# Six dense U rows a tile in the picking stage, and gathered dot products in three stages instead of one

## The reference, cut to what matters

```python
s = jnp.einsum('phcd,hckd->phck', qy, sub_keys)            # two scores tables a head
top_s, top_i = lax.top_k(s, PEER_TOPK)
cand_s = top_s[:, :, 0, :, None] + top_s[:, :, 1, None, :]
best_s, best_j = lax.top_k(cand_s.reshape(..., 256), 16)
gate = jax.nn.softmax(best_s, axis=-1)
act = jax.nn.gelu(jnp.einsum('pd,phkd->phk', xb, expert_u[experts]))
return jnp.einsum('phk,phkd->pd', gate * act, expert_v[experts])
```

## Time and profile before

| | us |
|---|---|
| median of 3 runs | 4415.63 (4413.09 to 4423.91) |
| profiled execution, whole | 4421.46 |
| span of its trace | 4419.7 |
| TensorE (matmul) busy | 3649.9 (83%) |
| VectorE busy | 2767.0 (63%) |
| ScalarE busy | 1112.5 (25%) |
| GpSimd busy | 825.4 (19%) |
| dot products L1116, 256 | 313.9, mean 1.226 each |
| gathers of U rows L1105, 256 | 317.3, mean 1.240 each |

### The profile page before, as it was taken

How to read it: one execution, slowest core, us unless ns; L and a number is a source line. 1 busy time by engine, 2 the same in 40 slices (tenths; PEclk the granted TensorE clock), 3 DMA queues, 4 the chain that set the end, 5 groups by cost and what they waited for, 6 DMA issues and landing times. The chain is left out here.

```text
span 4419.7 us, 61298 instructions
## 1 busy us (share of the span) xinstructions
PE 3649.9 (83%) x19108; PEld 3246.2 (73%) x19108; DVE 2767.0 (63%) x5265; ACT 1112.5 (25%) x1515; POOL 825.4 (19%) x900
## 2 busy tenths in 40 slices
PE   7499965555776588788788869999979999999996
PEld 1399965554655466788788869999977888888885
DVE  0322235655443566899777756666628888888887
ACT  0200014434321211222455542222222222222220
POOL 0000010111000000000000006666622222222221
PEclk9699986555777788898889989999989999999998
DMA  6222210000222100222365569999957777777775
GB/s 230 95 90 98 87 56 27 13 26 13 86 91 85 56 32 22 86 89 83 89 155 138 150 148 336 340 342 335 338 187 270 282 284 285 280 279 285 282 285 205
DMA packets 436796, 735.97 MB, mean 167 GB/s; under 512 B 222851, under 2 KB 274259, under 8 KB 433619
## 3 DMA queue, kind: packets, MB, share of 16 engines
q1 hardware_dynamic: 332052, 354.18, 24.2%
q0 software_dynamic: 98304, 368.10, 23.0%
q10 hardware_dynamic: 6336, 12.58, 0.8%
HBM read 605.75 MB, written 129.00 MB: 166 GB/s over the span
## 5 line engine op out<-in xcount | busy, mean ns | idle before, releaser
L329 PE MATMUL evo<-vhi,Hhi 128*128 128x512 f32 x1536 | 602.0, 392 | 47.0 <-DVE Hlo L1655 47.0
L330 PE MATMUL evo<-vlo,Hhi 128*128 128x512 f32 x1536 | 598.8, 390 | 0.0
L331 PE MATMUL evo<-vhi,Hlo 128*128 128x512 f32 x1536 | 598.4, 390 | 0.0
L329 PE MATMUL apar<-h2hi,auhir 128*128 128x384 f32 x1152 | 390.6, 339 | 53.2 <-DVEq L59 48.8
L1116 DVE SCALAR_TENSOR_TENSOR urow<-urow,nx 128x1024 f32<-128x1024 f32 x256 | 313.9, 1226 | 186.6 <-DMA urow<-in_expert_u_rows,fw_now 170.6
L1105 POOL DMA_INDIRECT vrow<-in_expert_v,fw_now x256 | 268.2, 1048 | 769.5 <-DVE acc L1125 757.8
L331 PE MATMUL apar<-h2hi,aulor 128*128 128x384 f32 x1152 | 386.3, 335 | 0.0
L330 PE MATMUL apar<-h2lo,auhir 128*128 128x384 f32 x1152 | 386.2, 335 | 0.0
L329 PEld LDWEIGHTS evo<-vhi,Hhi 128*128 128x128 f32 x1536 | 288.8, 188 | 119.5 <-issue 60.3
L1668 DVE TENSOR_TENSOR acc<-acc,evo 128x512 f32<-128x512 f32 x384 | 262.6, 684 | 167.4 <-PE evo L331 167.3
L1105 POOL DMA_INDIRECT urow<-in_expert_u_rows,fw_now x256 | 317.3, 1240 | 187.5 <-DVE urow L1116 87.2
(11 more groups left out here) (278 smaller groups left out, 7523.2 us busy)
## 6 DMA issues: line engine op xcount, KB each, us to landing
vraw<-in_expert_v SPq DMA_DIRECT2D x128, 512.0 KB
gates_dram<-gstage SPq DMA_DIRECT2D x12, 4096.0 KB, 21.9
ga<-ahead_dram SPq DMA_DIRECT2D x128, 384.0 KB, 5.3
gr<-gates_dram SPq DMA_DIRECT2D x128, 384.0 KB, 5.9
aurr<-in_expert_u POOLq DMA_DIRECT2D x72, 512.0 KB
ahead_dram<-ager SPq DMA_DIRECT2D x144, 192.0 KB
gwi<-in_w_in POOLq DMA_DIRECT2D x16, 1216.0 KB
proj_dram<-gyi SPq DMA_DIRECT2D x128, 152.0 KB, 1.8
```

The source lines that it names most:

```text
L329: pe.matmul(out, lhi, rhi, start=(k == 0), stop=False)
L330: pe.matmul(out, lhi, rlo, start=False, stop=False)
L331: return pe.matmul(out, llo, rhi, start=False, stop=(k == n - 1))
```

## The change

`ROWS_TILE` goes from 4 to 6, so 48 U rows lie in the picking stage and 56 are left for the last of the three stages; the gate stage keeps 24. Of the 256 items, 24 (four beside each dense tile) move to the picking stage, 48 (four a block) to the gate stage, and 184 stay, in 23 of 28 turns. The row buffers now exist in all three stages (two of them are halves of a tile of the norm stage).

```diff
-ROWS_TILE = 4
+ROWS_TILE = 6
 ROWS_BLOCK = 2
+ITEMS_BEST = DT * RING
+ITEMS_GATE = TD // 64 * RING
+ITEMS_REST = ITEMS - ITEMS_BEST - ITEMS_GATE
```

```diff
-                with pool.Fori(0, TT) as t:
-                    for j in range(R):
-                        A.load(pool, t * R + j, j % 2, row(t, j))
+                for j in range(2):
+                    A.load(pool, j, j, row(0, j))
+                for f in range(FEW):
+                    loads(f, range(R))
+                pool.wait_ge(index_done, FEW)
+
+                def pair(turn, last):
+                    for h in range(2):
+                        d = turn * 2 + h
+                        some = R - 2 if last and h else R
+                        few.choose(pool, d, h, d * RING)
+                        for i in range(RING):
+                            few.gather(pool, table, d, h, i)
+                            if i < some:
+                                loads(d + FEW, range(i, i + 1))
+                        loads(d + FEW, range(RING, some))
```

```diff
+                        if j == R // 2:
+                            act.wait_ge(bm_done, t + 1)
+                            act.activation(best[:, :, :], best[:, :, :], ACT.Exp).then_inc(be_done, 1)
...
+                    def dot(i):
+                        if one is None:
+                            few.dot_row(dve, (t + (-FEW)) * RING + i, i)
...
                                   + [dve.match_replace(cand2[:, h], best[:, h, 0:8], cand[:, h], NEG) for h in heads])
+                    cut(1)
+                    dot(0)
                     settle(dve, settled)
                     link.together([dve.max(best[:, h, 8:16], cand2[:, h]) for h in heads])
-                    cut(1)
                     settle(dve, settled)
                     link.together([dve.max_index(bj[:, h, 8:16], best[:, h, 8:16], cand2[:, h]) for h in heads])
+                    cut(2)
+                    dot(1)
...
                     link(dve.tensor_copy(rank[:, :, :], code[:, :, :]))
-                    cut(2)
...
                         link(dve.tensor_reduce(pick[:, c], eq[:, :, :, :].rearrange("p h k a -> p (h k) a"), AX, ALU.add))
+                        cut(3 + c)
+                        dot(2 + c)
...
-                    cut(3)
...
+                    cut(5)
```

```diff
+                    for half in range(2):
+                        b = turn * 2 + half
+                        batch = b + ITEMS_BEST // RING
+                        few.choose(pool, batch, half, batch * RING)
+                        for i in range(RING):
+                            few.gather(pool, table, batch, half, i)
+                            if i % 2 == 0 and not (last and half == 1):
+                                A.load(pool, b * 2 + (2 + i // 2), i // 2, b * 2 + (R0 + 2 + i // 2))
...
+                            if gi % RING == RING - 1:
+                                i = gi // RING
+                                few.dot_row(dve, b * RING + (ITEMS_BEST + i), i)
                             j, k = divmod(gi, PER)
-                            if k == 5 and not (last and half == 1 and j == ROWS_BLOCK - 1):
+                            if k == 4 and not (last and half == 1 and j == ROWS_BLOCK - 1):
                                 A.cut_low(link, b * 2 + (j + 1), 1 - j)
...
+                            if k == 0 and gi:
+                                A.gelu(act, b * 2 + (j - 1), 1)
+                            if k == 1 and not (last and half == 1 and j == ROWS_BLOCK - 1):
+                                A.cut_high(act, b * 2 + (j + 1), 1 - j, (b + j) * 16 + 16)
                             if k == 4:
                                 A.gelu(act, b * 2 + j, 0)
-                                if not (last and half == 1 and j == ROWS_BLOCK - 1):
-                                    A.cut_high(act, b * 2 + (j + 1), 1 - j, (b + j) * 16 + 16)
```

More of the change, by code:

```diff
@@ L1092, in __init__, with choose, gather, gather_all @@
         self.now_done = ctx.enter_context(nc.semaphore("fw_now_done"))
-    def gather(self, pool, table, first, batch, turn_batches, turn):
-        n = turn * (turn_batches * RING) + (first + batch * RING)
-        column = turn * (turn_batches * RING) + (first % ITEMS + batch * RING)
+    def choose(self, pool, batch, h, column):
         flat = self.index[:, :, :].rearrange("p s f -> p (s f)")
-        h = batch % 2
         pool.tensor_copy(self.now[:, h], flat[:, bass.ds(column, RING)]).then_inc(self.now_done, 1)
-        pool.wait_ge(self.now_done, turn * turn_batches + (first // RING + batch + 1))
+        pool.wait_ge(self.now_done, batch + 1)
+    def gather(self, pool, table, batch, h, i):
+        pool.wait_ge(self.row_used.sem, self.row_used.free(batch * RING + i))
+        settle(pool, self.settled)
+        pool.indirect_dma_start(self.ring[i], None, table, bass.IndirectOffsetOnAxis(ap=self.now[:, h, i:i + 1], axis=0)
+                                ).then_inc(self.row_in[i], 16)
+    def gather_all(self, pool, table, batch, h, column):
+        self.choose(pool, batch, h, column)
         for i in range(RING):
[L1103 to L1106, removed]
+            self.gather(pool, table, batch, h, i)
     def take(self, dve, n, i):
@@ L1124, in add_row @@
         at = acc[:, DT + i % FEW]
[L1125 removed]
+        dve.scalar_tensor_tensor(at, self.ring[i], flat[:, bass.ds(n - ITEMS, 1)], at, ALU.mult, ALU.add
                                  ).then_inc(self.row_used.sem, 1)
@@ L1227, in _, with loads @@
                 A.open(pool)
-                with pool.Fori(0, TT) as t:
-                    for j in range(R):
-                        A.load(pool, t * R + j, j % 2, row(t, j))
+                few.row_used.open(pool)
+                def loads(t, js):
+                    for j in js:
+                        A.load(pool, t * R + (j + 2), j % 2, row(t, j + 2))
+                for j in range(2):
[13 more added lines that the diff above has]
+                        loads(d + FEW, range(RING, some))
+                with pool.Fori(0, DT // 2 - 1) as turn:
+                    pair(turn, False)
+                pair(DT // 2 - 1, True)
             @block.sync
@@ L1335, in _, with gate_phase @@
                 turns(pe, tile)
-def gate_phase(nc, iT, jT, wT, gates, h2hi, h2lo, expert_u, ahead, keep):
+def gate_phase(nc, iT, jT, wT, gates, h2hi, h2lo, expert_u, ahead, few, table, keep):
     K = keep
@@ L1373, in _, with body @@
                     steps.open(pool)
-                with pool.Fori(0, NB) as b:
-                    for j in range(ROWS_BLOCK):
-                        A.load(pool, b * 2 + j, j, b * 2 + (R0 + j))
+                for j in range(ROWS_BLOCK):
+                    A.load(pool, j, j, R0 + j)
+                def body(turn, last):
+                    for half in range(2):
[6 more added lines that the diff above has]
+                                A.load(pool, b * 2 + (2 + i // 2), i // 2, b * 2 + (R0 + 2 + i // 2))
+                turns(pool, body)
             @block.vector
@@ L1476, in rest_phase @@
         A = Ahead(nc, ctx, sem, K, h2hi, h2lo, expert_u, ahead, "r", ROWS)
-        few.ring = ctx.enter_context(nc.sbuf_tensor("urow", [P, RING, D], F32))
         act_done = sem("few_act_done")
@@ L1499, in body @@
                         if rows:
-                            few.gather(pool, table, 0, p, BATCHES, turn)
+                            batch = turn * BATCHES + (BEFORE // RING + p)
+                            few.gather_all(pool, table, batch, p, batch * RING)
                 for p in range(2):
@@ L1579, in expert_phase @@
         Hhi, Hlo = sb("Hhi", [P, 2 * Q, TD], F32R), sb("Hlo", [P, 2 * Q, TD], F32R)
-        few.ring = sb("vrow", [P, RING, D])
+        vrow = sb("vrow", [P, RING, D])
+        few.ring = [vrow[:, i] for i in range(RING)]
         vo = [ctx.enter_context(nc.psum_tensor(f"evo{i}", [P, HALF], F32)) for i in range(BANKS)]
@@ L1620, in _ @@
                 with pool.Fori(0, GROUPS // 2) as turn:
-                    for batch in range(2 * EACH // RING):
-                        few.gather(pool, expert_v, ITEMS, batch, 2 * EACH // RING, turn)
+                    for k in range(2 * EACH // RING):
+                        done = turn * (2 * EACH // RING) + k
+                        few.gather_all(pool, expert_v, done + ITEMS // RING, k % 2, done * RING)
             @block.scalar
@@ L1763, in program @@
             few.h2 = nx[:, 4 - FEW:4]
+            urow = c1.enter_context(nc.sbuf_tensor("urow", [P, RING - 2, D], F32))
+            few.ring = [nx[:, 0], nx[:, 1], *(urow[:, i] for i in range(RING - 2))]
             norm_phase(nc, "2", x1, K.a2, K.mod[:, 24:32], h2hi, h2lo, nx, K)
```

22 lines of the change are left out of this document (10 added, 12 removed).

## The result

The changed kernel takes 4311.93 us (median of 4 runs, 4305.68 to 4316.54), beside 4414.36 (4408.75 to 4423.91) for the kernel before in runs on the same chip: a ratio of 0.976, interval 0.974 to 0.978. Predicted were 4314 us, so the forecast case came out. The profiled execution took 4316.54 us (span 4314.9), 104.9 less than the one before.

A forecast was written before the change was run, and what follows sets the result against it. It took VectorE to bound the picking stage, neither engine the gate stage (waits for ScalarE's high part), and gathers the remaining rows' pace. +102 - 60 - 144 = -102 from 4421.5 gives 4319.5, less 5.8 to the median: 4314 us, range 4283 to 4376.

The forecast's parts named there:

- forecast case: Whole kernel: the time lands between 4300 and 4335 us, around the predicted 4314; chance 0.50.
- Remaining rows: Last of the three stages: 18 fewer U rows with gathers at 8.9 us, two more without at 8.32; -144 us.
- Picking stage: Dense tiles held by a ring (cut 4, row 5, transposes, copies, next tile) at 55.8 us; +102 us with clock loss.
- the clock: Picking stage: the 3.0 us wait before row 4 may lower TensorE's clock, 0 to 1.1 us a tile; 3 us taken.
- The slack before cut 4: Picking stage: TensorE would wait 1.6 us for cut 4 anyway, absorbing that much of up to 2.7 us clock loss.
- Gate stage: Earlier `cut_high` removes the 3.0 us wait; VectorE with dots then sets 17.8 us a U row, was 20.3; -60 us.
- the loop's turns: Gate stage: loop turns stay and add 0.6 us to each U row's 17.2.
- Rival (a): Picking stage held by VectorE's and TensorE's lists, not the ring: 50.7 us a tile, 25 less, 4289; chance 0.14.
- Rival (b): Gate stage keeps its pace, as the wait moves or small idles lower the clock: -60 becomes 0, 4374; chance 0.18.
- Rival (c): Gate stage becomes DMA-bound, share 0.79, deciding once landing slips over 7 us; 4430 at 10 us a block; chance 0.06.
- Rival (d): Gate stage: GpSimd's work lengthens VectorE's operations through shared SBUF interfaces; 4386 at worst, 4350 at half; chance 0.07.
- Rival (e): Moved rows only shift work between stages that wait for TensorE; with the gate stage at 0, 4405; chance 0.05.

The follow-up runs named there:

- the half rows: Kernel before with last-stage gathers fetching 2 KB half rows, buffers cleared once, products written to a separate buffer: 4389.18 us, ratio 0.9932; full-row twin 4421.99 us.
- f1: Kernel before with only the gate stage's order changed, `cut_high` behind the second group and `cut_low` behind the fifth: 4312.96 us, ratio 0.9781.
- f4: Changed kernel with 16 instead of 48 dots in the gate stage (first four blocks), the other 32 moved to the last stage: 4285.66 us, ratio 0.9721.
- f3: Changed kernel with all four dots of a picking-stage dense tile placed behind cut 4: 4292.43 us, ratio 0.9724.
- f9: Changed kernel with the copies of a picking-stage tile's transposes made behind cut 0 of the next tile: 4289.16 us, ratio 0.971.
- f2: Changed kernel with the gate stage's `cut_high` and `cut_low` put back to their old places: 4360.93 us, ratio 0.9883.
- f7: Changed kernel with four blocks a turn instead of two in the gate loop, on every engine that loops there: 4297.17 us, ratio 0.9729.

## Why the prediction was right

- **Remaining rows, -144 predicted, -146 measured**: from first to last low part 621.6 us before (2647.6 to 3269.2), 475.6 after. 18 x - 16.6 = 146 gives 9.03 us for each of the 18 U rows with gathers that left. Read off the stage as the prediction did, the pace is 8.92 before and (3104.0 - 2699.2 - 5.6)/45 = 8.87 after (the stage's first dot starts at 2699.2): the 2 us beyond the forecast came from the rows that stayed. That the pace would stay rested on the gathers beside a row being as before; the half rows show the reason, bytes.
- **Picking stage, +102 predicted, +97 measured**: first candidates to last copies 431.7 us against 433 from the sum, plus 3 for the clock. The waits before row 4 came (2.31 to 2.74), and the clock fell behind four of the five, yet it cost 0 to 0.1 us a tile: row 4 to transposes is 18.26 to 18.35 us in these tiles, 18.28 where it stayed up. The slack before cut 4, which the prediction put at 1.6 and counted against only part of the loss, took in all of it; that was the mis-sized term. (Its upper end for this stage, +125, is also a slip: 102 and 5 x 4 are 122.) The tiles: 47.5, 50.2, 57.4, then three of 55.8 and one of 55.3, and in the last the copies end 53.9 after its start. The start cost less than 49.9 + 2.7, and tile 2 more than 50.7: TensorE, behind from the first two tiles, was already what its copies waited for. The three together are 155.1 against 153.2.
- **Gate stage, -60 predicted, -55.6 measured**: from the first copy into `gstage` to the end 484.0 before, 428.4 after. VectorE's list is 17.05 where I had 17.2, and the loop's turns are 20.9 us in all where I took 24 x 0.6 = 14.4. The terms within -60 are better told apart by f1: the same distance is 386.1 there, so the order gives -98 and the 48 dots, with what they make of the loop's jumps, +42, which is 0.9 each. The prediction never wrote these two down separately, and so missed that the first is the gain and that a dot costs three times as much here (0.9) as in the last stage (0.3 in f4). Sum of the parts by measurement: 97.1 - 55.6 - 146.0 = -104.5, and the span lost 104.8.
- **The moved work alone**: +97 - 146 + 42 = -7, and the timed difference between f1 and the full change is too small to tell.
- **Rival (a), lists instead of ring**: not so here, tiles are 55.8; but f3 and f9 come near it by edits, and their gains (16 and 22 us by the ratios, 19 and 23 by the medians) are most of its 25.
- **Rival (b), the gate stage keeps its pace**: no; where TensorE idles in small pieces the clock stays at 1.00 (f1's window). In the changed kernel's gate stage the half clock comes back only behind the jumps.
- **Rival (c), DMA-bound gate stage**: share 0.78 in its window, near the 0.79 reckoned, landing 24.4 instead of 21.9, a slip of 2.5 where 7 was the point from which it decides. Not reached.
- **Rival (d), contention**: the cut takes 1.224 us beside 69 us of GpSimd's work, 1.226 beside 13; the dots 1.225, as in the earlier trace rows. The rule that the prediction weighed would have lengthened both; this kernel doesn't show it.
- **Rival (e), shifted work**: its number, 4405, was wrong, since it put the gate stage at 0. Its thought was right for the part of the change that it spoke of: rows and dots moved between stages that all wait for TensorE, the DMA or VectorE net about nothing.

The total is nearer than its parts deserve: errors of -5, +4 and -2 cancel in part. What can't be settled is what makes the clock fall. It isn't the length of the wait alone: behind the picking stage's waits of 2.73 and 2.74 us it fell three times and stayed up once, and behind those of 2.74 to 2.77 in f2's gate stage it did either, too.

## What to carry to other kernels

When a change bundles several edits, put a price on each by itself, not on each stage: here one stage's number hid a gain of 98 us from the order of two calls and a loss of 42 from the work put beside it. A short wait repeated in an in-order list can be worth more than it shows (3.0 us seen, 4.3 gained in f1), when another engine's work queues behind it and the clock falls; where the waiting engine's own list is next in line it isn't (2.0 seen, 2.2 gained, f2 against the changed kernel). And an operation's place decides its price: the same dot cost 1.3 us ahead of the cut that TensorE waits for, almost nothing behind it, 0.9 in a stage that VectorE fills, 0.3 in one that waits for bytes.

## What the runs showed of the hardware

- A jump back of the gate stage's loop cost 5.2 us a turn with dots (22 against 17.05; f7 took three away for 15.7 us), of which about 3 are idle time of VectorE marked "issue" and the rest its waits for TensorE at clock 0.50 behind it. Where VectorE has slack, without dots, it cost 1.2 (17.1 against 15.95 in f1). The Trainium skill (Advanced Engine Details and Errata, ISA Cache) tells of an instruction cache of two lines; whether a refill of it is this idle time no run here shows.
- Halving a gathered row's bytes at the same count of gathers brought the DMA share from 0.95 to 0.75 and the last stage's U row to TensorE's own pace, (3235.6 - 2647.7)/71 = 8.28 us.
- Behind TensorE waits of one length the granted clock either fell or didn't. In the changed kernel's picking stage it was 0.50 at some time behind three waits of 2.73 and 2.74 us (first matmuls at 1976.08, 2087.68 and 2143.51) and 1.00 behind another of 2.74 (2031.92). In f2's gate stage it stayed 1.00 behind waits of 2.75 at 2260.93 and 2544.08, and fell to 0.50 behind 2.77 at 2280.14 and 2.76 at 2300.05.
- Such a slow stretch cost nothing where TensorE would have waited anyway (18.33 us against 18.28 in the picking stage), and 2.6 us where VectorE waited for TensorE (0.73 + 1.91 behind the jump at 2302).
